# Weighted sum of values in the second attention layer: fp32 operands against rounded parts and remainders

## The reference

```python
q = _rope(_rmsnorm(q, q_norm_g), cos, sin)
k = _rope(_rmsnorm(k, k_norm_g), cos, sin)
_, sel = lax.top_k(score, topk)                  # 64 keys for each token, by the indexer
s = jnp.einsum('btgrd,btkgd->btgrk', qg, k_sel).astype(jnp.float32) * attn_scale
s = jnp.where(valid[:, :, None, None, :], s, -jnp.inf)
p = jax.nn.softmax(s, axis=-1)
o = jnp.einsum('btgrk,btkgd->btgrd', p.astype(v.dtype), v_sel)
return o.reshape(B, Q_BLOCK, N_HEADS * HEAD_DIM) # then out @ w_o
```

## Time and profile before

| | |
|---|---|
| median of 3 runs | 2215.14 us (2214.73 to 2215.17) |
| profiled execution | 2214.63 us, of which the span from first to last instruction is 2212.9 |
| busy: TensorE, its weight loads, VectorE, ScalarE | 2206.6, 1930.9, 1484.2, 1176.9 us |
| value sums of layer 1 (records `psum<-prt,v_cur`) | from 1304.0 to 1405.7 us in the span |

### The profile page before, as it was taken

The page is one execution under the profiler, slowest core; times in us unless marked ns, Lnnn a source line. Parts: engine busy times, 40 slices in busy tenths (PEclk is TensorE's granted clock), DMA queues, the critical chain, the costliest instruction groups (busy, mean ns, idle before and its releaser), DMA issues.

```text
span 2212.9 us, 34732 instructions
## 1 busy us (share of the span) xinstructions
PE 2206.6 (100%) x12450; PEld 1930.9 (87%) x12450; DVE 1484.2 (67%) x1753; ACT 1176.9 (53%) x1409; POOL 14.9 (1%) x21
## 2 busy tenths in 40 slices
PE   9999999999999999999999999999999999999999
PEld 8888898888888888888899888888888888888887
DVE  7666556677777777555578888667777777774443
ACT  7565555555555555444455466555555555553333
POOL 0000000000000000000020000000000000000000
PEclk9999999999999999999999999999999999999999
DMA  7555545656555556565566544456565556566664
GB/s 271 166 171 174 171 163 181 199 181 195 184 198 181 194 185 195 189 190 190 189 211 199 180 154 140 159 185 194 179 200 179 199 180 199 180 196 202 200 198 136
DMA packets 113828, 411.54 MB, mean 186 GB/s; under 512 B 12768, under 2 KB 13536, under 8 KB 113760
## 3 DMA queue, kind: packets, MB, share of 16 engines
q1 hardware_dynamic: 112320, 406.70, 56.6%
q10 hardware_dynamic: 1008, 2.30, 0.3%
q0 software_dynamic: 432, 1.57, 0.2%
HBM read 408.42 MB, written 2.10 MB: 186 GB/s over the span
## 4 chain that ended last, share of the span: by engine, by line
PE 99%; DMA 0%; SPq 0%; DVE 0%; ACT 0%; issue 0%; DVEq 0%
PE psum L1303 99%; DMA raw<-w_all 0%; PE psum L1618 0%; PE psum L1554 0%; DVE w_lo L748 0%; ACT w_hi L289 0%; SPq L237 0%; SPq L235 0%; DVE upad L824 0%; SPq L236 0%; SPq L234 0%; DVEq L83 0%
## 5 line engine op out<-in xcount | busy, mean ns | idle before, releaser
L748 DVE TENSOR_TENSOR w_lo<-raw,w_hi 128x1024 fp32r<-128x1024 f32 x769 | 935.4, 1224 | 675.3 <-ACT w_hi L289 669.5
L1303 PE MATMUL psum<-xg,w_hi 128*128 128x512 f32 (+1 forms) x3936 | 1357.4, 391 | 1.6 <-DVE xg L759 0.8
L289 ACT CAST w_hi<-raw 128x1024 fp32r<-128x1024 f32 x770 | 802.8, 1049 | 767.6 <-PE psum L1303 764.2
L1303 PE MATMUL psum<-xg,w_lo 128*128 128x256 f32 (+1 forms) x3920 | 1089.0, 278 | 0.0
L1303 PEld LDWEIGHTS psum<-xg,w_hi 128*128 128x128 f32 x3936 | 735.4, 187 | 157.0 <-issue 2.5
L1303 PEld LDWEIGHTS psum<-xg,w_lo 128*128 128x128 f32 x3920 | 740.9, 189 | 2.7 <-issue 2.2
L1303 PE MATMUL psum<-hid,w_hi 128*128 128x512 f32 x704 | 244.1, 391 | 0.0
L1303 PE MATMUL psum<-w_hi,hid 128*128 128x512 f32 x704 | 217.8, 390 | 0.0
L1303 PE MATMUL psum<-hid,w_lo 128*128 128x256 f32 x704 | 197.1, 280 | 0.0
L1303 PE MATMUL psum<-att,w_hi 128*128 128x512 f32 x512 | 178.8, 393 | 0.0
L1303 PEld LDWEIGHTS psum<-hid,w_hi 128*128 128x128 f32 x704 | 131.6, 187 | 28.9
(11 more groups left out here) (174 smaller groups left out, 1058.7 us busy)
## 6 DMA issues: line engine op xcount, KB each, us to landing
raw<-w_all SPq DMA_DIRECT2D x770, 512.0 KB, 3.7
xres<-x_in SPq DMA_DIRECT2D x3, 512.0 KB, 9.2
cst<-consts_in ACTq DMA_DIRECT2D x2, 768.0 KB, 7.0
raw<-w_all SPq DMA_DIRECT2D x2, 256.0 KB, 3.6
xres<-x_in SPq DMA_DIRECT2D x2, 256.0 KB, 4.1
out_t<-part POOLq DMA_DIRECT2D x1, 512.0 KB, 7.0
out_t<-conv POOLq DMA_DIRECT2D x1, 512.0 KB, 7.0
out_t<-gates POOLq DMA_DIRECT2D x1, 512.0 KB, 7.1
```

Source lines behind the costliest of these rows:

```text
L289: act.copy(w_hi[:, c % RING, :], raw[:, c % RING, :]).then_inc(hi_ready, 1)
L748: dve.tensor_tensor(w_lo[:, c % RING, :], raw[:, c % RING, :], f32(w_hi[:, c % RING, :]), ALU.subtract).then_inc(lo_ready, 1)
L1303: return pe.matmul(o, lhsT, rhs, start=start, stop=True, skip_group_check=True)
```

## The change

The values and the turned probabilities are each held as a rounded part (fp32r) and a remainder, as the other products of the kernel are, and the weighted sum is three fp32r products of each: rounded by rounded, rounded values by the probabilities' remainder, the values' remainder by rounded probabilities. ScalarE makes the rounded parts with the copies that it made before. VectorE makes the remainders: `v_low1`, four times, from `v_all`, and `p_low`, eight times, straight from the turned probabilities in PSUM. Since the mask may not overwrite these before VectorE has read them, `seed_scores` now waits for `p_low`, through `pt_ready`, which VectorE raises; a new semaphore `pt_hi` tells VectorE that the rounded part is there. The squares `usq` move into two of the four tiles of `conv`.

```diff
-        v_cur = sb("v_cur", [P, 2, P], F32, l1)
+        v_cur = sb("v_cur", [P, 2, 2, P], F32R, l1)
-        usq = sb("usq", [P, 2, T], F32, l1)
+        usq = conv[:, 0:2, :]
-        prt = sb("prt", [P, 2, 384], F32, l1)
+        prt = sb("prt", [P, 2, 2, 384], F32R, l1)
...
             def prt_copy(t):
                 act.wait_ge(tr_ready, t + 1)
-                act.copy(prt[:, :, :], psum[:, 6:8, 0:384]).then_inc(pt_ready, 1)
+                act.copy(prt[:, 0, :, :], psum[:, 6:8, 0:384]).then_inc(pt_hi, 1)
                 if not isinstance(t, int) or t < PAIRS - 1:
                     act.wait_ge(pt_ready, t + 1)
                     seed_scores()
...
-                act.copy(v_cur[:, :, :], v_all[:, :, bass.ds(g * P, P)]).then_inc(vcur_ready, 1)
+                act.copy(v_cur[:, 0, :, :], v_all[:, :, bass.ds(g * P, P)]).then_inc(vcur_hi, 1)
...
+            def v_low1(g, n_v):
+                dve.wait_ge(vcur_hi, n_v)
+                dve.tensor_tensor(v_cur[:, 1, :, :], v_all[:, :, bass.ds(g * P, P)], f32(v_cur[:, 0, :, :]), ALU.subtract).then_inc(vcur_ready, 1)
+
+            def p_low(t):
+                dve.wait_ge(pt_hi, t + 1)
+                dve.tensor_tensor(prt[:, 1, :, :], psum[:, 6:8, 0:384], f32(prt[:, 0, :, :]), ALU.subtract).then_inc(pt_ready, 1)
...
                     if e == 0 and t_soft is not None:
                         maxes(t_soft)
+                        if v_g is not None:
+                            v_low1(v_g, v_g + 1)
                         normalise(t_soft)
...
+                    if e == 2 and t_av is not None:
+                        p_low(t_av)
                     split(base + e + RING, i, per)
...
             def l1_head(e):
                 if e in (0, 3):
                     maxes(6 + e // 3)
                     if e == 0:
+                        v_low1(3, 4)
                         rope_prev(18, "q", 10, ("cos",))
                     normalise(6 + e // 3)
                 if e == 1:
                     rope_prev(18, "q", 10, (1,))
+                    p_low(6)
+                if e == 4:
+                    p_low(7)
...
-                mm(o, v_cur[:, 0, :], prt[:, :, 0:T], True)
-                mm(o[:, :, P:T], v_cur[:, 1, :], prt[:, :, T:384]).then_inc(av_ready, 1)
+                for n, (vp, pp) in enumerate(THREE):
+                    mm(o, v_cur[:, vp, 0, :], prt[:, pp, :, 0:T], n == 0)
+                for vp, pp in THREE:
+                    last = mm(o[:, :, P:T], v_cur[:, vp, 1, :], prt[:, pp, :, T:384])
+                last.then_inc(av_ready, 1)
```

More of the change, by code:

```diff
@@ L190, in build @@
         att_hi, att_ready = sem("att_hi"), sem("att_ready")
-        v1_ready, vcur_ready = sem("v1_ready"), sem("vcur_ready")
+        v1_ready, vcur_hi, vcur_ready, pt_hi = sem("v1_ready"), sem("vcur_hi"), sem("vcur_ready"), sem("pt_hi")
         tables_ready = sem("tables_ready")
@@ L1217, in _, with block1 @@
             dve.tensor_tensor(wi_t[0:2 * NH, TI:T], psum[0:2 * NH, 3, 0:T - TI], wi_t[0:2 * NH, TI:T], ALU.add).then_inc(wi_sum, 1)
-            def block1(B, i, per, par, nb, prev, t_score, t_soft, t_av, base, extra=None):
+            def block1(B, i, per, par, nb, prev, t_score, t_soft, t_av, base, extra=None, v_g=None):
                 for e in range(4):
@@ L1276, in _ @@
             with dve.Fori(0, 3) as i:
-                block1(13 + 2 * i, i, 8, 0, 5 + 2 * i, ("q", 4 + 2 * i), None, 2 * i, 2 * i, L1_Q + 8)
+                block1(13 + 2 * i, i, 8, 0, 5 + 2 * i, ("q", 4 + 2 * i), None, 2 * i, 2 * i, L1_Q + 8, v_g=i)
                 block1(14 + 2 * i, i, 8, 1, 6 + 2 * i, ("q", 5 + 2 * i), None, 2 * i + 1, 2 * i + 1, L1_Q + 12)
```

## The result

The changed kernel takes 2219.78 us (median of 12 runs, 2218.86 to 2221.09) against 2214.89 (12 runs, 2214.26 to 2215.17): +4.89 us, a ratio of 1.0023 [1.0016, 1.0031]. The profiled execution took 2219.2 us (span 2217.4), 4.57 more than before's 2214.63. The forecast was 2219.8, between 2215.8 and 2221.6.

A forecast was written before the change was run, and what follows sets the result against it. TensorE bounds the kernel (99% of the chain that ended last). A 5.18 us delay less two savings of 0.24 gives +4.70: 2214.63 becomes 2219.3, and the median, 0.5 above, 2219.8 us; range 2215.8 to 2221.6.

The forecast's parts named there:

- The loop: Blocks 13 to 18: p_low, hand-over, seed, rounding of piece 3, split 3, next p_low; 15.79 us a block against 15.28.
- Pair 6 and 7: First output group: value sum of t = 6 starts 5.18 us late, t = 7 does not wait; each saves 0.24.
- TensorE's saving: Each value sum falls from 1.29 to 1.05 us, saving 0.24; of eight savings six vanish in waits, two are kept.
- Values' remainder: VectorE's v_low1, four times 0.43 us, hidden in its 1.79 us wait for ScalarE's exponentials; costs nothing.
- TensorE's waits: Sign: weight loads idle some 0.8 us for VectorE in blocks 13 to 18, above 1.5 at t = 6, none at t = 7.
- split 3: VectorE's split of piece 3 in each block; idle time ahead stays about as long (1.05 us before), ended by ScalarE's rounding.
- The wait without a loop: Rival: seeding does not hold up piece 3, only direct waits for p_low remain; +1.2 us, 2216.3; chance 0.13.
- The hidden remainder: Rival: p_low fits beside TensorE in VectorE's 1.05 us idle per block; only -1.9 us remains, 2213.2; chance 0.08.
- The clock: Rival: waits in each block lower TensorE's clock; one block at 1.2 instead of 2.4 GHz gives 2235 us; chance 0.05.

The follow-up runs named there:

- Experiment 8: Changed kernel with the mask left out, so ScalarE seeds no scores and nothing there waits for p_low; 2217.09 us, 1.0012 of the kernel before.
- experiments 3: Changed kernel plus a fourth product, remainder by remainder, in each value sum, so more TensorE work; 2221.69 us, 1.0033 of the kernel before.
- 11: Changed kernel with TensorE's part undone: fp32 tiles and two fp32 matmuls, VectorE's remainders and all waits kept; 2220.06 us, 1.0026 of the kernel before.
- experiment 5: Changed kernel with p_low moved ahead of the last rope product in VectorE's queue; 2214.72 us, 1.0001 of the kernel before.
- experiment 7: Changed kernel, p_low ahead of last rope product (at t = 6, of rope's sum), copy before norm scaling there, 512/256-column matmuls in turn; 2214.0 us, 0.9998 of before.
- experiments 4: Changed kernel with p_low between the rope's sine products and its sum, at t = 6 ahead of the last product; 2214.98 us, 1.0006 of before.
- 6: Changed kernel with the value sum's matmuls of 512 and 256 columns in turn; 2219.8 us, 1.0023 of the kernel before.
- 10: The kernel of experiment 7 plus an unused fp32 matmul of 256 columns behind the last value sum; 2215.44 us, 1.0003 of the kernel before.
- 12: The kernel before with only the squares' buffer moved into conv; 2215.01 us, 1.0001 of the kernel before.
- experiment 1: Changed kernel, ScalarE first copying the probabilities to SBUF, rounding from there and seeding at once, VectorE subtracting from that copy; 2220.54 us, 1.0025 of before.
- 2: Changed kernel with VectorE doing p_low's subtraction twice, once into a scratch tile; 2228.05 us, 1.0063 of the kernel before.
- 9: The kernel of experiment 7 plus an unused fp32 matmul of 512 columns behind the last value sum; 2216.1 us, 1.0003 of the kernel before.

## Why the prediction was right

**The loop held, term by term.** Forecast 0.95 + 0.04 + 0.73 + 1.08 + 12.99 = 15.79 us; measured, in rows, 0.99 + 0.74 + 1.07 + 13.00 = 15.80, and 15.79 over five blocks. p_low took 0.95 us, as in the row of its shape. Experiment 8 shows that it is a loop and not one wait, experiments 3 and 11 that TensorE has no part in it.

**Pair 6 and 7.** The stage began 0.25 us earlier in the profile after (1303.49 against 1303.74). Less that, t = 6 was forecast for 1397.72 and stands at 1397.62. Pair 7's sum stands at 1409.18 against 1404.41: +4.77, +0.25 for the earlier start, -0.24 for its own saving, 4.78 against the forecast's 4.70. It does not wait.

**TensorE's saving.** A sum that does not wait takes 1409.18 to 1410.23 = 1.05 us, as forecast from the projection's pairs. So the saving is 0.24. The estimate of 0.32 from the four passes that the Trainium skill gives for true fp32 ("FP8 and Floating Point Precision", "TensorE Precision Notes") is not what the trace shows. Where a sum waits, it takes 1.16 (1304.67 to 1305.83), which costs nothing in the loop.

**Values' remainder.** 0.43 us, and the wait for exponentials shrinks from 1.79 to 1.32: hidden.

**TensorE's waits.** The forecast named the weight loads: idle for some 0.8 us in each block, above 1.5 at t = 6, none at t = 7. Their timeline for the values gives 1.10 at t = 0, 0.65 to 0.82 from t = 1 to 5, 1.66 at t = 6 and none at t = 7:

```profile
1336.25 1.12 PEld L1319 LDWEIGHTS psum<-prt,v_cur 128*128 128x128 f32 x6 [0.82 <-issue]
...
1397.62 1.12 PEld L1319 LDWEIGHTS psum<-prt,v_cur 128*128 128x128 f32 x6 [1.66 <-DVE prt L1187]
...
1409.06 1.12 PEld L1319 LDWEIGHTS psum<-prt,v_cur 128*128 128x128 f32 x6
```

Only at t = 6 does this view name VectorE as what ended the wait; for the others the matmuls' rows above name it. Those show less idle time (0.34 to 0.51 from t = 1 to 5), as they count from the modelled end of the matmul in front.

**What was off.** One size that changes no sum: VectorE idles 0.72 us ahead of split 3, not about 1.05, since split 2 starts later in its block, while split 3 follows the loop. And that the median is met to 0.02 us is luck: 8 of its 12 runs lie at 2218.86 to 2219.92 and 4 at 2220.6 to 2221.09, for a reason that the forecast did not know.

**The rivals.** The wait without a loop is what experiment 8 shows once the seed is gone; its price was too low, +1.2 forecast and +2.4 measured, of which 0.7 comes from its five steps (p_low's starts against the forecast's value sums), 76.58 us together where 1380.70 - 1304.84 = 75.86 were forecast. The hidden remainder is wrong as the change stands; in experiment 5 it holds for the blocks, though its -1.9 us did not come (0.0 by the medians): the slot had to open 0.87 us earlier, and the rope product that was moved behind p_low takes 0.60 of that (1318.96 to 1319.56 there), enough for no wait to show from t = 1 to 5. The clock stayed at 1.00 in the window above. The Trainium skill's case of short pauses that make the clock go back and forth ("TensorE: Matmul & The Clock Gate", "A second HAM failure mode: psum-queue depth-cycling") did not come up here: with waits of 0.34 to 1.34 us, one per block of 15.8, the windows of the stage from 1300 to 1430 us all have a granted clock of 1.00.

## What to carry to other kernels

When a change gives an instruction a new wait, look at what stands behind it in its engine's queue, follow that from engine to engine, and see whether it comes back to the start: a closed loop that is longer than a turn of the bottleneck becomes the bottleneck, though none of its engines is busy all the time (here VectorE for 63.96 and ScalarE for 48.48 of 76.20 us). Inside such a loop, work taken off the old bottleneck counts for nothing (experiments 3 and 11). Before giving up a change for that, look for the one place in the queue where the new instruction stands ahead of work that can wait: here one rope product moved behind it was worth the whole 5 us.

## What the hardware showed that was not expected

TensorE runs the projection's pair of matmuls (512 and 256 columns) at one of two distances, at the same granted clock of 1.00. The timelines of experiment 5 and experiment 7 over the same work of the output projection:

```profile
1429.93 0.39 PE L1321 MATMUL psum<-att,w_hi 128*128 128x512 f32 x1
1430.16 0.28 PE L1321 MATMUL psum<-att,w_lo 128*128 128x256 f32 x1
1430.28 0.39 PE L1321 MATMUL psum<-att,w_hi 128*128 128x512 f32 x1
```

```profile
1429.85 0.40 PE L1322 MATMUL psum<-att,w_hi 128*128 128x512 f32 x1
1430.09 0.28 PE L1322 MATMUL psum<-att,w_lo 128*128 128x256 f32 x1
1430.21 0.40 PE L1322 MATMUL psum<-att,w_hi 128*128 128x512 f32 x1
```

One step is too small to read; the whole stretch is not. Between the last value sum and the next fp32 product stand 248 pairs. From the start of the second to the start of the last are 85.27 or 85.28 us in the profiles of before, of the change and of experiments 4, 5, 6, 8, 10, 11 and 12 (0.3467 a pair), and 86.92 or 86.93 in those of experiments 1, 2, 3, 7 and 9 (0.3533): 1.64 us. The windows there have the clock at 1.00 for both, with 118 matmuls in 20 us of the changed kernel and 115 in 20 us of experiment 1:

```profile
1430.00:1450.00 20.00, 20.00 (x118) 17.62 (x117) 11.81 (x13) 11.40 (x14) 0.00 (x0) 1.00 0.59 199
```

```profile
1429.70:1449.70 20.00, 20.00 (x115) 17.38 (x114) 11.20 (x13) 10.82 (x13) 0.00 (x0) 1.00 0.59 185
```

This is the size of the gap between the two groups of runs, and in the profiled executions it accounts for what experiments 1, 2 and 3 took beyond their stage. That it makes the groups in the runs without a profile is argued from the size, not shown. Nor is it all of the spread: the profiled executions of experiments 8 and 11 ran at the lower distance and lie 1.3 us above the fastest run of their kernels. They reached the stage late, with ScalarE's copy (L642) of t = 0 at 1302.69 and 1302.32 against 1301.69 before, for a reason that is open too. What selects the distance stays open: it is not the order of the matmuls alone (6 and 7 have the same order, and their profiles the two distances), and an fp32 product behind the sum does not reset it (9). To judge by its times, the kernel before ran at the lower one nearly always.
